# A decoder layer whose sigmoid gates move from classical products inside the merge loop to 14 Strassen units after the gated linear units

## Chip, core and metric

One core of a Trainium2 chip runs the whole layer in one launch. The metric is the device time in microseconds (us). Lower is better.

## What is computed

The layer takes x (1, 512, 2048) in float32. Cut to what matters here:

```
h = rms_norm(x, norm_mix_pre)
q, k, v, u, gate_a, gate_s = jnp.split(h @ w_in, IN_SPLITS, axis=-1)     # gates: 2048 columns each
...
attn_branch = attn.reshape(bsz, s, ATTN_OUT_WIDTH) @ w_attn_up           # 512 -> 2048
y = jax.nn.gelu(s5_ssm(u, ...))                                          # 1024 wide
ssm_branch = (y @ w_glu_v) * jax.nn.sigmoid(y @ w_glu_g)                 # 1024 -> 2048, twice
merged = jax.nn.sigmoid(gate_a) * attn_branch + jax.nn.sigmoid(gate_s) * ssm_branch
x = x + rms_norm(merged @ w_out, norm_mix_post)                          # 2048 -> 2048
h = rms_norm(x, norm_ffn_pre)
f = (jax.nn.silu(h @ w_ffn_gate) * (h @ w_ffn_up)) @ w_ffn_down
return x + rms_norm(f, norm_ffn_post)
```

## The kernel before

**Precision.** Every large product is done three times over: each operand is split into a high part (`_hi`, written by ScalarE as an fp32r copy) and the rest (`_lo`, written by VectorE as raw minus high), and TensorE accumulates hi*hi, hi*lo and lo*hi. The activations stay in SBUF as `a_hi`, `a_lo` (16 tiles of 128 features by 512 tokens) and, for the gated linear units, `y_hi`, `y_lo` (8 tiles). The weights stream from DRAM.

**Pieces.** A piece is 512 KB of weights (four row tiles by 256 columns for `piece_f`; two by 512 for `piece_t`). SP loads it into one of four `raw` slots (`load`), ScalarE splits it (`split_hi`: it waits until piece m-2 is done, since the high parts have two slots), VectorE follows (`split_lo`), and TensorE runs 24 matmuls that stream 512 columns each. So splits of a piece are made while TensorE works on the piece ahead of it. All orders are written out by hand, one list per engine, tied by semaphores; each engine works off its list in order.

**Merge.** Output features are taken in 8 pairs of tiles (256 features, all 512 tokens). Pair 0 of both gates (8 pieces, `B_G0`), the attention output for all pairs (8 pieces, `B_AU`, left in `mrg`) and four pieces of the gated linear unit (`B_Y0`) come first. A loop over `it` = 1 to 7 then runs 12 pieces per pair: four for gate_a, four for gate_s, four for the two halves of the gated linear unit. `gate_glu` takes the sigmoids on ScalarE, `merge` and `merge_attention` multiply and add on VectorE in place in `mrg`. The last turns split `mrg` into `a_hi`, `a_lo` for w_out (`mrg_split_hi`, `mrg_split_lo`), 32 pieces of `piece_t` (`B_WO`).

**Strassen units.** The feed-forward part already does 10 of its 11 column groups as units: 256 output features by 512 tokens by 2048 inputs, as 7 products (`unit_product`, p = 0 to 6) of 8 inner tiles by 3 matmuls that stream 256 columns each: 168 matmuls. Sums of weight quarters are made on VectorE (`block_sum`, four a unit), split operands by `operand_hi` on ScalarE and `operand_lo` on VectorE (seven a unit, into a ring of four slots), the output quarters are put together from PSUM by five small VectorE operations (p = 3, 5, 6 and the next unit's p = 0) and two ScalarE ones. The sums of the activations are made once ahead (`sums`). Even units go with `w_ffn_gate`, odd ones with `w_ffn_up`; each odd one's product is taken by `gate_times_up` in the next unit.

## Time and profile before

| | |
|---|---|
| median of three runs | 2783.3 us (2783.28 to 2784.62) |
| the profiled execution, its own time | 2784.49 us |
| its span from first to last instruction | 2782.7 us |
| TensorE busy | 2733.8 us, 98% |
| VectorE, ScalarE, GpSimd busy | 1307.5, 901.8, 370.2 us |
| mean granted TensorE clock | 0.994 of full |

The page is that of one profiled execution. Busy times of TensorE overlap, so what counts for it is the distance of the starts of consecutive matmuls, and where it sat idle. The other engines' busy shares tell only whether they could be in the way; whether they are is read where an engine waits.

### The profile page before, as it was taken

What the parts mean: (1) busy time and instruction counts of PE and PEld (TensorE: products, weight loads), DVE (VectorE), ACT (ScalarE), POOL (GpSimd) and SP (SyncE); (2) the same over time, 40 slices, a digit from 0 to 9 for tenths busy, and PEclk for the clock granted to TensorE, in tenths of its full rate; (3) what the DMA queues carried; (4) which work ended last, traced back from release to release, by engine and by line L of the source; (5) the groups of instructions that cost most, each with busy time, mean ns of one, the idle gap of its engine ahead of it and who ended that gap; (6) DMA issues with size and microseconds to landing.
All of it is one profiled execution on the core that took longest, in us unless ns stands there. A gap on an engine that the chain in (4) does not pass through costs nothing.

```text
span 2782.7 us, 42515 instructions
## 1 busy us (share of the span) xinstructions
PE 2733.8 (98%) x16733; PEld 2424.5 (87%) x16733; DVE 1307.5 (47%) x1458; ACT 901.8 (32%) x1122; POOL 370.2 (13%) x579
## 2 busy tenths in 40 slices
PE   7999999999999999999799999999999999999998
PEld 6888888888888888888589999999999998888887
DVE  5232332233322223332476777777777773334334
ACT  5222322232322222232333434343433342223223
POOL 5958017761000000000000000000000000000000
PEclk9999999999999999999899999999999999999999
DMA  6444643246233332343334333333334246444443
GB/s 174 141 135 131 126 132 94 92 82 154 91 98 98 98 94 95 98 174 98 105 112 132 106 126 107 118 124 106 127 106 136 98 133 229 141 143 147 147 144 132
DMA packets 256750, 342.46 MB, mean 123 GB/s; under 512 B 22656, under 2 KB 212160, under 8 KB 255520
## 3 DMA queue, kind: packets, MB, share of 16 engines
q1 hardware_dynamic: 232232, 287.89, 32.6%
q0 software_dynamic: 7152, 35.07, 4.7%
q10 hardware_dynamic: 17288, 18.40, 1.9%
q8 instruction: 56, 0.92, 0.1%
q14 instruction: 22, 0.18, 0.0%
HBM read 309.40 MB, written 31.92 MB: 123 GB/s over the span
## 4 chain that ended last, share of the span: by engine, by line
PE 96%; DVE 2%; ACT 1%; issue 1%; DMA 0%; POOL 0%; ACTq 0%; DVEq 0%
PE ps L380 12%; PE ps L382 12%; PE ps L384 12%; PE ps L553 10%; PE ps L551 10%; PE ps L554 10%; PE ps L589 5%; PE ps L587 5%; PE ps L588 5%; PE ps L441 2%; PE ps L439 2%; PE ps L440 2%; PE ps L420 2%; PE ps L424 2%; PE ps L422 2%
## 5 line engine op out<-in xcount | busy, mean ns | idle before, releaser
L368 DVE TENSOR_TENSOR w_lo<-raw,w_hi 128x1024 fp32r<-128x1024 f32 x240 | 308.8, 1287 | 745.6 <-ACT w_hi L364 745.2
L364 ACT ACTIVATE w_hi<-raw 128x1024 fp32r<-128x1024 f32 x240 | 254.1, 1059 | 765.7 <-PE ps L384 532.5
L380 PE MATMUL ps<-a_hi,w_hi 128*128 128x512 f32 x1136 | 445.4, 392 | 1.2 <-issue 1.2
L382 PE MATMUL ps<-a_lo,w_hi 128*128 128x512 f32 x1136 | 442.7, 390 | 0.0
L384 PE MATMUL ps<-a_hi,w_lo 128*128 128x512 f32 x1136 | 442.6, 390 | 0.0
L380 PEld LDWEIGHTS ps<-a_hi,w_hi 128*128 128x128 f32 x1136 | 213.4, 188 | 47.5 <-issue 3.7
L384 PEld LDWEIGHTS ps<-a_hi,w_lo 128*128 128x128 f32 x1136 | 213.3, 188 | 44.3
L382 PEld LDWEIGHTS ps<-a_lo,w_hi 128*128 128x128 f32 x1136 | 213.5, 188 | 43.1
L551 PE MATMUL ps<-a_hi,w_hi 128*128 128x256 f32 x640 | 181.4, 284 | 0.0
L553 PE MATMUL ps<-a_lo,w_hi 128*128 128x256 f32 x640 | 181.4, 283 | 0.0
L554 PE MATMUL ps<-a_hi,w_lo_b 128*128 128x256 f32 x640 | 181.4, 283 | 0.0
L551 PE MATMUL ps<-a_hi,w_hi_b 128*128 128x256 f32 x640 | 181.4, 283 | 0.0
L553 PE MATMUL ps<-a_lo,w_hi_b 128*128 128x256 f32 x640 | 181.4, 283 | 0.0
L554 PE MATMUL ps<-a_hi,w_lo 128*128 128x256 f32 x640 | 181.4, 283 | 0.0
L564 DVE TENSOR_TENSOR f_lo<-f_raw,f_hi 128x512 fp32r<-128x512 f32 x84 | 58.2, 693 | 260.9 <-ACT f_hi L560 260.9
L560 ACT ACTIVATE f_hi<-f_raw 128x512 fp32r<-128x512 f32 x84 | 53.0, 631 | 309.3 <-PE ps L589 309.3
L553 PE MATMUL ps<-s_lo,w_hi_b 128*128 128x256 f32 x480 | 136.1, 284 | 0.0
L554 PE MATMUL ps<-s_hi,w_lo_b 128*128 128x256 f32 x480 | 136.1, 283 | 0.0
L553 PE MATMUL ps<-s_lo,w_hi 128*128 128x256 f32 x480 | 136.1, 283 | 0.0
L554 PE MATMUL ps<-s_hi,w_lo 128*128 128x256 f32 x480 | 136.1, 283 | 0.0
L551 PE MATMUL ps<-s_hi,w_hi 128*128 128x256 f32 x480 | 136.1, 283 | 0.0
L551 PE MATMUL ps<-s_hi,w_hi_b 128*128 128x256 f32 x480 | 136.1, 283 | 0.0
(320 smaller groups left out, 6375.4 us busy)
## 6 DMA issues: line engine op xcount, KB each, us to landing
raw<-in_w_in SPq DMA_DIRECT2D x152, 512.0 KB, 3.6
raw<-in_w_ffn_gate SPq DMA_DIRECT2D x88, 512.0 KB, 4.6
raw<-in_w_ffn_down SPq DMA_DIRECT2D x88, 512.0 KB, 3.7
raw_b<-in_w_ffn_up SPq DMA_DIRECT2D x80, 512.0 KB, 5.2
f_raw<-f_d SPq DMA_DIRECT2D x88, 256.0 KB, 2.7
raw<-in_w_out SPq DMA_DIRECT2D x32, 512.0 KB, 3.8
f_d<-f_t ACTq DMA_DIRECT2D x22, 512.0 KB, 2.8
raw<-in_w_glu_v SPq DMA_DIRECT2D x16, 512.0 KB, 3.4
```

Of the source, the lines that this page charges most:

```text
L364: nc.scalar.activation(w_hi[:, m % 2, :], raw[:, m % 4, :], ACT.Copy).then_inc(hi_ready, 1)
L368: nc.vector.tensor_tensor(w_lo[:, m % 2, :], raw[:, m % 4, :], w_hi[:, m % 2, :].bitcast(F32), ALU.subtract).then_inc(lo_ready, 1)
L380: nc.tensor.matmul(o, wh[:, k, cols], x_hi[:, kt0 + k, :], start=first and k == 0, stop=False, skip_group_check=halves)
L382: nc.tensor.matmul(o, wh[:, k, cols], x_lo[:, kt0 + k, :], start=False, stop=False, skip_group_check=halves)
L384: mm = nc.tensor.matmul(o, wl[:, k, cols], x_hi[:, kt0 + k, :], start=False, stop=last and k == 3, skip_group_check=halves)
L551: nc.tensor.matmul(o, wh[:, k, :], X_HI[p][:, k, :], start=p < 4 and k == 0, stop=False, skip_group_check=True)
L553: nc.tensor.matmul(o, wh[:, k, :], X_LO[p][:, k, :], start=False, stop=False, skip_group_check=True)
L554: mm = nc.tensor.matmul(o, wl[:, k, :], X_HI[p][:, k, :], start=False, stop=k == KT // 2 - 1, skip_group_check=True)
L564: nc.vector.tensor_tensor(dst, f_raw[:, n % 4, :], hi.bitcast(F32), ALU.subtract).then_inc(f_lo_ready, 1)
L587: nc.tensor.matmul(o, f_hi[n % 2][:, toks], wh[:, d, :], start=first, stop=False)
L588: nc.tensor.matmul(o, f_hi[n % 2][:, toks], wl[:, d, :], start=False, stop=False)
L589: mm = nc.tensor.matmul(o, f_lo[n % 2][:, toks], wh[:, d, :], start=False, stop=last)
```

## The change

Pair 0 of the gates stays classical. All 32 pieces of the gated linear unit now run in a row after the attention output; their results go pair by pair through `sig_g` to DRAM (`gl_d`), and the attention output (`mrg`, pairs 1 to 7) goes to DRAM (`au_d`) once, both by GpSimd's queue. In the gaps VectorE and ScalarE make the activation sums for Strassen (`gate_sums`, `gate_sum_hi`), partly in the memory of `mrg`. The seven other pairs of both gates then run as 14 units (`MIX`): even j is gate_a, odd j gate_s. In p = 2 of the odd unit the attention chunk `au_c`, read back from DRAM, is scaled by sigmoid(gate_a) (`merge_attention`); in p = 2 of the unit after it the chunk `gl_c` is scaled by sigmoid(gate_s) and added (`merge_ssm`); the sum goes from `au_c` to DRAM (`m_d`), and only when that has landed is the next `au_c` read. In the last unit `mrg` is read back in two transfers (2 MB and 1.5 MB) as its memory comes free, and the last pair is put into `mrg` straight from VectorE. The output banks of w_out change places. The feed-forward units keep their code, now with `FFN` as the parameter and other semaphore counts.

```diff
-B_WO = B_MRG + 7 * 12
+B_WO = B_Y0 + 4 * 8
 B_FF = B_WO + 32
 B_DN = B_FF + 16
-UNITS = 4 * (FFG - 1)
-DN_USED = 2 * (FFG - 1)
+MIX_UNITS = 2 * 7
+UNITS = MIX_UNITS + 4 * (FFG - 1)
+DN_USED = MIX_UNITS // 2 + 2 * (FFG - 1)
 PROD0 = 4
 LO0 = 8
...
-MRG_RUNS = ((0, 4), (4, 8), (8, 12), (12, 14), (14, 16))
+MRG_RUNS = ((0, 2), (2, 4), (4, 8), (8, 12), (12, 14), (14, 16))
 
...
-            for k in range(4):
-                load(sp, B_Y0 + k, 0, (w_gv, w_gg)[k // 2], 4, 4 * P * (k % 2), 0, 256)
-            with sp.Fori(2, 9) as it:
-                for k in range(12):
-                    if k < 8:
-                        src = (w_in, 4, 4 * P * (k % 4), 256 * it + (GA_COL, GS_COL)[k // 4] - 256, 256)
-                    else:
-                        src = ((w_gv, w_gg)[k // 2 - 4], 4, 4 * P * (k % 2), 256 * it - 256, 256)
-                    load(sp, B_MRG + k - 24, 3 * it, *src)
+            for it in range(8):
+                for k in range(4):
+                    load(sp, B_Y0 + 4 * it + k, 0, (w_gv, w_gg)[k // 2], 4, 4 * P * (k % 2), 256 * it, 256)
+            with sp.Fori(0, 3) as g:
+                for j in range(4):
+                    load_unit(sp, MIX, g, j, w_in, 512 * g + (GA_COL, GS_COL)[j % 2] + 256 * (j // 2 + 1))
+            for j in range(2):
+                load_unit(sp, MIX, 3, j, w_in, (GA_COL, GS_COL)[j] + 256 * 7)
+            sp.wait_ge(unit_lo, LO0 + 7 * (MIX_UNITS - 1))
             with sp.Fori(0, 2) as it:
                 for k in range(16):
                     load(sp, B_WO + k, 4 * it, w_out, 2, 2 * P * (k % 8), 1024 * it + 512 * (k // 8), 512)
...
             pe.wait_ge(au_copied, 8)
             pe.wait_ge(gelu_lo, SSM // P)
-            for k in range(4):
-                piece_f(pe, B_Y0 + k, 0, k // 2 + 2, y_hi, y_lo, 4 * (k % 2), k % 2 == 0, k % 2 == 1)
-            with pe.Fori(1, 8) as it:
-                for k in range(12):
-                    if k < 8:
-                        if k % 4 == 0:
-                            pe.wait_ge(gated, START - 2 + 3 * it + k // 4)
-                        piece_f(pe, B_MRG + k - 12, 3 * it, k // 4, a_hi, a_lo, 4 * (k % 4), k % 4 == 0, k % 4 == 3)
-                    else:
-                        if k == 8:
-                            pe.wait_ge(merge_step, START - 2 + 4 * it)
-                        if k == 10:
-                            pe.wait_ge(gated, START + 3 * it)
-                        piece_f(pe, B_MRG + k - 12, 3 * it, k // 2 - 2, y_hi, y_lo, 4 * (k % 2), k % 2 == 0, k % 2 == 1)
-            pe.wait_ge(gated, START + 23)
+            for it in range(8):
+                for k in range(4):
+                    if it >= 2 and k == 0:
+                        pe.wait_ge(gl_made, it - 1)
+                    if it >= 2 and k == 2:
+                        pe.wait_ge(gated, START + it + 1)
+                    piece_f(pe, B_Y0 + 4 * it + k, 0, 2 * ((it + 1) % 2) + k // 2, y_hi, y_lo, 4 * (k % 2), k % 2 == 0,
+                            k % 2 == 1)
+            with pe.Fori(0, 3) as g:
+                for j in range(4):
+                    for p in range(7):
+                        unit_product(pe, MIX, g, j, p)
+            for j in range(2):
+                for p in range(7):
+                    unit_product(pe, MIX, 3, j, p)
+            pe.wait_ge(c12_made, START + MIX_UNITS - 1)
+            pe.wait_ge(c21_made, START + MIX_UNITS - 1)
             with pe.Fori(0, 2) as it:
                 for k in range(16):
-                    if k in (0, 2, 4, 6, 7):
-                        pe.wait_ge(mrg_lo, (k + 1) // 2 + 1)
+                    if k in (0, 1, 2, 4, 6, 7):
+                        pe.wait_ge(mrg_lo, (0, 1, 2, 4, 6, 7).index(k) + 1)
                     if k == 8:
-                        pe.wait_ge(merge_step, START + 32)
+                        pe.wait_ge(m_made, 7)
+                        pe.wait_ge(c11_read, START + MIX_UNITS)
+                        pe.wait_ge(c12_made, START + MIX_UNITS)
+                        pe.wait_ge(c21_made, START + MIX_UNITS)
                     if k % 8 == 0:
                         pe.wait_ge(o_copied, START - 1 + 2 * it + k // 8)
-                    piece_t(pe, B_WO + k, 4 * it, 4 * (k // 8), a_hi, a_lo, 2 * (k % 8), k % 8 == 0, k % 8 == 7)
...
+                if k >= 8:
+                    c = (k - 8) // 12
+                    if k - 7 - 12 * c in (4, 6, 7, 10):
+                        gate_sum_hi(c, (4, 6, 7, 10).index(k - 7 - 12 * c))
+            act.wait_ge(piece_done, B_WO - 1)
+            operand_hi(act, MIX, 0, 0, 0)
+            act.wait_ge(piece_done, B_WO)
+            operand_hi(act, MIX, 0, 0, 1)
+            operand_hi(act, MIX, 0, 0, 2)
+            gate_glu(7)
...
+            for j in range(2):
+                for p in range(7):
+                    mix_product(3, j, p, False, j == 1)
+            split_hi(act, B_WO + 1, 0)
+            for part in range(2):
+                gate_sigmoids(MIX_UNITS - 1, 1, part)
+            for i in (2, 3, 4):
+                mrg_split_hi(i)
+            split_hi(act, B_WO + 2, 0)
+            mrg_split_hi(5)
...
+            def glu(it):
+
+                dve.wait_ge(gated, START + it + 3)
+                step = tt(sig_g[:, :], pair(2 * ((it + 1) % 2)), sig_g[:, :], ALU.mult)
+                step.then_inc(gl_made, 1)
+                if it == 0:
+                    dve.wait_ge(gl_made, 1)
+                    tt(sig_s[:, :], sig_g[:, :], sig_s[:, :], ALU.mult).then_inc(merge_step, 1)
+                    dve.wait_ge(merge_step, START + 2)
+                    tt(m0, m0, sig_s[:, :], ALU.add).then_inc(merge_step, 1)
...
+            def merge_ssm(g, j, out):
+
+                u = MIX.at(g, j)
+                dve.wait_ge(gl_in, 32 * g + 16 * (j // 2 + 1))
+                dve.wait_ge(gate_sig, 2 * u + 2)
+                dve.wait_ge(c11_read, START + u + 1)
+                tt(gl_c[:, :, :], gl_c[:, :, :], sg[1][:, :, :], ALU.mult).then_inc(gl_scaled, 1)
+                dve.wait_ge(gl_scaled, 2 * g + (j // 2 + 1))
+                dve.wait_ge(au_scaled, 2 * g + (j // 2 + 1))
+                tt(out, au_c[:, :, :], gl_c[:, :, :], ALU.add).then_inc(m_made, 1)
+
+            def merge_attention(g, j):
+
+                u = MIX.at(g, j)
+                dve.wait_ge(au_in, 32 * g + 16 * (j // 2 + 1))
+                dve.wait_ge(gate_sig, 2 * u)
+                dve.wait_ge(c11_read, START + u)
+                tt(au_c[:, :, :], au_c[:, :, :], sg[0][:, :, :], ALU.mult).then_inc(au_scaled, 1)
+
...
-                        merge_attention(it)
-            for k in range(1, 13):
-                split_lo(dve, B_MRG - 12 + k, 21)
-                if k <= 3:
-                    merge(6, k)
-                if k == 8:
-                    merge_attention(7)
-                if k >= 9:
-                    mrg_split_lo(k - 9)
-            for k in range(1, 33):
+            dve.wait_ge(gs_lo_ready, 8)
+            block_sum(MIX, 0, 0, 1)
+            operand_lo(dve, MIX, 0, 0, 0)
+            block_sum(MIX, 0, 0, 3)
+            operand_lo(dve, MIX, 0, 0, 1)
+            block_sum(MIX, 0, 0, 2)
+            glu(7)
+            for j in range(4):
...
+                for p in range(7):
+                    mix_product(3, j, p, False, j == 1)
+            mix_c21(MIX_UNITS - 1, 1)
+            split_lo(dve, B_WO + 1, 0)
+            mrg_split_lo(2)
+            merge_ssm(3, 1, mrg[:, KT - 2:KT, :])
+            mrg_split_lo(3)
+            mrg_split_lo(4)
+            split_lo(dve, B_WO + 2, 0)
+            mrg_split_lo(5)
+            for k in range(3, 33):
                 split_lo(dve, B_WO + k, 0)
-                if k <= 3:
-                    merge(7, k)
-                if k == 4:
-                    mrg_split_lo(4)
                 if k in (9, 17, 25):
                     out_gain((k - 9) // 8)
...
 
 
-            pool.wait_ge(mrg_lo, 5)
+            pool.wait_ge(au_copied, 8)
+            pool.dma_start(au_d[:, 2:KT, :], mrg[:, 2:KT, :]).then_inc(au_stored, 16)
+            pool.wait_ge(merge_step, START + 3)
+            pool.dma_start(m_d[:, 0:2, :], mrg[:, 0:2, :]).then_inc(m_stored, 16)
+            for it in range(1, 8):
+                pool.wait_ge(gl_made, it + 1)
+                pool.dma_start(gl_d[:, 2 * it:2 * it + 2, :].rearrange("p a n -> p (a n)"), sig_g[:, :]
+                               ).then_inc(gl_stored, 16)
+            for it in range(1, 8):
+                kts = slice(2 * it, 2 * it + 2)
+                if it > 1:
+                    pool.wait_ge(m_made, it - 1)
+                    pool.dma_start(m_d[:, 2 * it - 2:2 * it, :], au_c[:, :, :]).then_inc(m_stored, 16)
+                    pool.wait_ge(m_stored, 16 * it)
+                else:
+                    pool.wait_ge(gs_lo_ready, 8)
+                    pool.wait_ge(au_stored, 16)
+                pool.dma_start(au_c[:, :, :], au_d[:, kts, :]).then_inc(au_in, 16)
+                pool.wait_ge(gl_stored, 16 * it)
+                pool.dma_start(gl_c[:, :, :], gl_d[:, kts, :]).then_inc(gl_in, 16)
+            pool.wait_ge(product, PROD0 + 7 * MIX_UNITS - 5)
+            pool.dma_start(mrg[:, 0:8, :], m_d[:, 0:8, :]).then_inc(mrg_in[0], 16)
+            pool.wait_ge(product, PROD0 + 7 * MIX_UNITS - 4)
+            pool.dma_start(mrg[:, 8:14, :], m_d[:, 8:14, :]).then_inc(mrg_in[1], 16)
+
```

Two places on VectorE, as the program lists them. In names, buffer numbers left out, `w_lo` and `mix_lo_b` are the four slots of the ring for low parts; what stands in brackets is what the operation waits for. The first place is where the classical pieces end and the units begin, now (the row at the top splits the last piece of the gated linear unit):

```order
L417 TENSOR_TENSOR w_lo<-raw,w_hi 128x1024 [waits hi_ready]
L1797 TENSOR_TENSOR gs_lo_145<-gs_tmp_150,gs_hi_142 128x1024 [waits gs_hi_ready]
L1846 TENSOR_TENSOR mix_t_sum<-raw 128x1024 [waits landed1,landed0,gs_lo_ready]
L566 TENSOR_TENSOR w_lo<-raw,w_hi 128x1024 [waits unit_hi]
L1849 TENSOR_TENSOR raw<-raw 128x8x128 [waits landed3,landed2]
L566 TENSOR_TENSOR w_lo<-raw,w_hi 128x1024 [waits unit_hi]
L1852 TENSOR_TENSOR raw<-raw 128x8x128 [waits t_made]
L1778 TENSOR_TENSOR sig_g<-ps,sig_g 128x1024 [waits gated]
L566 TENSOR_TENSOR mix_lo_b<-raw,mix_hi_b 128x1024 [waits unit_hi] x2
```

The product of the last gated linear unit (L1778) stands between the second operand's low part and the third's. ScalarE's list at the same place, from the high part of operand 0 to that of operand 3, has its sigmoid (L1278) there too:

```order
L561 ACTIVATE w_hi<-raw 128x1024 [waits landed1,product,landed0,piece_done]
L561 ACTIVATE w_hi<-raw 128x1024 [waits landed3,product,landed2,piece_done]
L561 ACTIVATE mix_hi_b<-raw 128x1024 [waits product,t_made]
L1278 ACTIVATE sig_g<-ps 128x1024 [waits piece_done,gl_stored]
L561 ACTIVATE mix_hi_b<-raw 128x1024 [waits product,t_made]
```

The sigmoid comes behind operand 2's high part there, while on VectorE the product that needs it comes ahead of operand 2's low part. The last place is VectorE at the start of w_out. Before, the splits of w_out's weights (L368) and the last merge's steps and splits took turns:

```order
L1682 TENSOR_TENSOR a_lo<-mrg,a_hi 128x1024 [waits mrg_hi]
L368 TENSOR_TENSOR w_lo<-raw,w_hi 128x1024 [waits hi_ready]
L1653 TENSOR_TENSOR sig_g<-ps,sig_g 128x1024 [waits gated]
L368 TENSOR_TENSOR w_lo<-raw,w_hi 128x1024 [waits hi_ready]
L1656 TENSOR_TENSOR sig_g<-sig_g,sig_s 128x1024 [waits merge_step]
L368 TENSOR_TENSOR w_lo<-raw,w_hi 128x1024 [waits hi_ready]
L1659 TENSOR_TENSOR mrg<-mrg,sig_g 128x1024 [waits merge_step]
```

Now (from the split of w_out's first piece, the first L417, on; the second L417 splits its second piece, the third its third):

```order
L417 TENSOR_TENSOR w_lo<-raw,w_hi 128x1024 [waits hi_ready]
L1859 TENSOR_TENSOR sg_157<-mix_u_159,ps 128x256 [waits product]
L417 TENSOR_TENSOR w_lo<-raw,w_hi 128x1024 [waits hi_ready]
L1939 TENSOR_TENSOR a_lo<-mrg,a_hi 128x2048 [waits mrg_hi]
L1867 TENSOR_TENSOR gl_c<-gl_c,sg_157 128x1024 [waits c11_read,gate_sig,gl_in]
L1870 TENSOR_TENSOR mrg<-au_c,gl_c 128x1024 [waits au_scaled,gl_scaled]
L1939 TENSOR_TENSOR a_lo<-mrg,a_hi 128x2048 [waits mrg_hi]
L1939 TENSOR_TENSOR a_lo<-mrg,a_hi 128x1024 [waits mrg_hi]
L417 TENSOR_TENSOR w_lo<-raw,w_hi 128x1024 [waits hi_ready]
```

Five operations of VectorE stand between the low parts of w_out's second and third piece, where before one stood between two neighbours.

## Rows read from the trace of the kernel before

**Rows 1.** The page: span and busy time of each engine.

```profile
span 2782.7 us, 42515 instructions
...
PE 2733.8 (98%) x16733; PEld 2424.5 (87%) x16733; DVE 1307.5 (47%) x1458; ACT 901.8 (32%) x1122; POOL 370.2 (13%) x579
```

**Rows 2.** Busy time by window: merge from the first B_Y0 piece; feed-forward units.

```profile
717.50:1196.40 478.90, 478.85 (x2112) 396.82 (x2113) 147.76 (x120) 119.08 (x113) 0.00 (x0) 1.00 0.31 96
1488.50:2294.90 806.40, 806.40 (x6721) 806.36 (x6721) 604.40 (x659) 325.91 (x403) 0.00 (x0) 1.00 0.36 119
```

**Rows 3.** Waits of TensorE from 718 to 1370 us: total, times, longest.

```profile
PE ps L380 <- ACT mrg L1208: 1.1, 1, 1.1
```

**Rows 4.** Timeline of VectorE: end of an odd unit, an even unit from 1851.4.

```profile
1840.10 0.42 DVE L1812 TENSOR_TENSOR u_s<-p_s,ps 128x256 f32<-128x256 f32 x1 [3.04 <-PE ps L554]
...
1855.91 1.22 DVE L1791 TENSOR_TENSOR f_t<-f_t,f_sg 128x1024 f32<-128x1024 f32 x1
1857.05 1.22 DVE L519 TENSOR_TENSOR w_lo<-t_sum,w_hi 128x1024 fp32r<-128x1024 f32 x1
1860.35 0.42 DVE L1812 TENSOR_TENSOR u_s<-p_s,ps 128x256 f32<-128x256 f32 x1 [2.08 <-PE ps L554]
```

**Rows 5.** Timeline of ScalarE in the odd unit from 1831.3.

```profile
1834.22 0.62 ACT L1301 ACTIVATE f_sg<-f_sg 128x512 f32<-128x512 f32 x1
...
1835.70 0.40 ACT L1301 ACTIVATE f_sg<-f_sg 128x256 f32<-128x256 f32 x1
```

**Rows 6.** Timeline of TensorE and ScalarE where product 3 of a unit ends.

```profile
1822.61 0.28 PE L551 MATMUL ps<-a_hi,w_hi_b 128*128 128x256 f32 x1
...
1822.83 1.06 ACT L514 ACTIVATE w_hi<-raw 128x1024 fp32r<-128x1024 f32 x1 [4.71 <-PE ps L554]
```

**Rows 7.** Chain of waits: VectorE's split, then 0.14 us until TensorE starts.

```profile
709.37 1.23 DVE w_lo L368
710.60 0.14 issue
```

**Rows 8.** Operations on mrg: durations in ns, min/median/max.

```profile
L1208 ACT ACTIVATE mrg<-ps x8: 1023/1025/1026, 667.6 to 716.5; 128x1024 f32<-128x1024 f32 x8
...
L1659 DVE TENSOR_TENSOR mrg<-mrg,sig_g x8: 1216/1218/1219, 752.8 to 1209.8; 128x1024 f32 x6, 128x1024 f32<-128x1024 f32 x2
L1227 ACT ACTIVATE a_hi<-mrg x5: 1044/1902/1907, 1176.7 to 1213.9; 128x2048 fp32r<-128x2048 f32 x3, 128x1024 fp32r<-128x1024 f32 x2
L1682 DVE TENSOR_TENSOR a_lo<-mrg,a_hi x5: 1217/2291/2293, 1178.7 to 1215.2; 128x2048 fp32r<-128x2048 f32 x3, 128x1024 fp32r<-128x1024 f32 x2
```

**Rows 9.** DMA issues: count, KB each, median us from issue to landing.

```profile
h_r<-h_d POOLq DMA_DIRECT2D x8, 512.0 KB, 14.7
...
x_d<-x POOLq DMA_DIRECT2D x1, 4096.0 KB, 11.4
x_b<-x_d POOLq DMA_DIRECT2D x1, 4096.0 KB, 17.8
```

**Rows 10.** Windows (us, PE, PEld, DVE, ACT, POOL busy, TensorE's clock, DMA).

```profile
1370.00:1371.00 1.00, 0.64 (x3) 0.19 (x1) 0.00 (x0) 0.32 (x1) 0.00 (x0) 1.00 0.55 194
...
1372.00:1373.00 1.00, 0.00 (x0) 0.00 (x0) 0.00 (x0) 1.00 (x4) 0.00 (x0) 0.89 0.00 0
1373.00:1374.00 1.00, 0.00 (x0) 0.00 (x0) 0.83 (x3) 0.98 (x3) 0.00 (x0) 0.50 0.00 0
...
1396.00:1397.00 1.00, 1.00 (x8) 1.00 (x7) 0.90 (x2) 0.83 (x2) 0.00 (x0) 0.66 0.01 0
```

**Rows 11.** Timeline of TensorE at half clock, and the restart at 1392.6.

```profile
25.10 0.41 PE L403 MATMUL ps<-a_lo,w_hi 128*128 128x256 f32 x1
25.32 0.41 PE L405 MATMUL ps<-a_hi,w_lo 128*128 128x256 f32 x1
...
1392.62 8.83 PE L709 MATMUL ps<-ident,o_t 128*128 128x128 f32 x61 [0.72 <-DVE o_t L1719]
```

475 lines of the change are left out of this document (322 added, 153 removed).

## The prediction

> **What bounds the kernel now.** First the page's busy times: TensorE is busy 2733.8 of 2782.7 us, VectorE 47%, ScalarE 32% [rows 1]. The reader is to see that only TensorE can set the time as a whole; a change helps by giving it less to stream, and hurts by making it wait. Then the busy time by window, for the stage that is changed: from 717.50 to 1196.40 us, TensorE runs 2112 matmuls of 512 columns without a gap, one every 478.85/2112 = 0.2267 us. VectorE is busy 147.8 us of that, DMA 31% [rows 2]. Its waits in this stage come to 1.1 us in all, once, for ScalarE's last copy of the attention output [rows 3]; the change leaves that one in place. The same view of the feed-forward units gives 6720 matmuls of 256 columns in 806.4 us: 0.1200 us each, again without a gap, with VectorE at 604.4/806.4 = 75% [rows 2]. So both forms of work are in the trace, at full clock.
>
> **The change part by part.** *Removed and added products.* A gate's pair of tiles took 4 pieces, 96 matmuls of 0.2267: 21.77 us. As a unit it takes 168 of 0.1200: 20.16 us, the same for any unit, since 40 of them took 806.4. 14 x 1.61 = 22.5 us less. The 32 pieces of the gated linear units are the same matmuls as before; only their order changes.
> The Trainium skill's page "TensorE: Matmul & The Clock Gate", section "Back-to-back issue gap", has a matmul cost its columns over 2.4 GHz and 2.5 ns: 109 ns for 256 columns, 216 for 512. By that a unit would be 18.3 us, four pieces 20.7, and 14 of them would save 33 us. The rows show 120 and 227 ns, so the sum goes by them.
>
> *Work that TensorE hides.* Ahead of the units VectorE does 24 sums of 1024 elements and ScalarE 8 copies, at most one each a piece, behind the piece's split. A VectorE operation of that size starts 1.14 us after the one ahead of it (1855.91, 1857.05) and takes 1.22 [rows 4]; a piece on TensorE is 24 x 0.2267 = 5.44 us, and split, sum and the pair's product come to 3.6. Nothing. If the cover went, a sum would cost 1.14 us a time.
> In the units, VectorE has what it has in the feed-forward units plus, in p = 2, one operation of 1.22 in an odd unit (there was none) and two in an even one (there was one, L1791). What they eat into is its idle time ahead of p = 3: 3.04 us in an odd unit, 2.08 in an even one [rows 4]. 3.04 - 1.2 leaves 1.8. In the even one the sigmoids come in: ScalarE now takes them in every unit, 0.62 and 0.40 [rows 5], which puts operand 4's high part some 0.6 later, and the add must wait for the scaling, so 2.08 - 1.2 - 0.2 leaves near 0.6 at best and near nothing at worst. VectorE then starts p = 3's sum when product 3 is done, as now, 2.2 us before TensorE needs it (the sum ends at 1860.77; the unit began at 1822.61 - 4 x 2.88 + 2 x 20.16 = 1851.41 [rows 6], its product 4 starts 11.52 later). Nothing, in all 14 units.
>
> *Two places where the cover is gone.* **The first unit.** Call T0 the end of the last classical piece. The high part of operand 1 goes into the slot that piece used, operand 2's where `y_hi` lay, so both come after T0. ScalarE sees an end of products about 0.25 after the next matmul could start (1822.83 against 1822.61 [rows 6], somewhat more with 512 columns). ScalarE 0.25 to 1.31 (1.05 for 1024 elements, 0.96 from start to start of two); VectorE's low part to 2.57, its third sum to 3.71; ScalarE's operand 2 to 4.88, its sigmoid to 5.81 (1.03, as L1208 [rows 8]); VectorE's product of the gated linear unit to 7.07, and only then operand 2's low part, to 8.22. From such an end to TensorE's start is 0.14 [rows 7]: 8.36, where product 2 was due at 2 x 2.88 = 5.76. A stall of 2.6 us. Behind that row wait TensorE and VectorE's operand 3, which is done at 9.4, before product 3.
> **w_out's third piece.** Call T1 the end of the last unit. ScalarE: split of the second piece to 1.31, two sigmoids to 2.15, the 2048-element high part to 3.95 (1.90 [rows 8]). VectorE: 1.35 to 2.58, low part 3.97 to 6.26 (2.29), scaling and adding the last pair to 8.67, a low part of 2048 and one of 1024 to 12.02, and then the third piece's split, to 13.17. TensorE starts it at 13.3; it was due at T1 + 10.88. A stall of 2.4 us. The fourth piece is due 5.44 later and needs two more operations: no stall. Before, single operations stood between the splits and nothing waited. Together 5.0 us; as bounds, 0 if work TensorE has queued covers it, 7 if each chain is a microsecond longer than its sum.
>
> *The clock.* TensorE's last matmul before the end of w_out ends at 1370.64. The window from 1372 shows 0.89, the one from 1373 0.50 of the clock, that is 1.2 GHz: it fell some 2.1 us into the idle time, after a long dense stretch. It came back in the window from 1396, 4.1 us after TensorE's long run began at 1392.62 [rows 10, 11]. Both stalls are a little longer than 2.1. At half clock, matmuls of 256 columns start every 0.21 us instead of 0.12 [rows 11]; 4.1 us of that lose 4.1 x (1 - 0.12/0.21) = 1.8 us. The other end of the bound is nothing, as the 1.1 us stall at 716 cost nothing more. I take one fall of the two, 1.8; the bounds are 0 and 3.6.
>
> *DMA.* Through GpSimd's queue go 3.5 MB at the start of the linear units, then 0.5 MB a pair, and 1.5 MB for each pair of units. On it 4096 KB left SBUF in 11.4 us and came back in 17.8 with 1 MB ahead of it [rows 9]. The slots run three pieces ahead (16 us), so a weight load that lands ten us later still makes it. The last unit's 2 MB read is issued at its 6.0 us and is wanted at 14.6; half of 11.4 and half of 17.8 are 5.7 and 8.9, so it lands at 11.7 to 14.9: nothing to 0.6 us. Nothing.
>
> *Sum.* -22.5 + 5.0 + 1.8 = -15.7 us. The profiled execution took 2784.49, so its like would take 2768.8, with a span of 2767.0; the median of the runs is 1.2 below it, and 2783.3 - 15.7 = 2767.6.
>
> **The rivals.** Under 0.2% (5.6 us) is about what a measurement of this kernel can't tell from no change.
> *No stall shows (12%).* Queued work covers both places, or the clock holds and one of them is hidden. For it: in all units so far TensorE never waited. Against it: the sums above have no slack. 2783.3 - 22.5 = 2760.8, up to 2763.
> *The reload is late (10%).* ScalarE's wait for `mrg` stands in front of w_out's first split. If the 2 MB take as long per byte as 512 KB of `h_r` did amid other traffic, 14.7 [rows 9], they land 6 us late: 2767.6 + 6 = 2774.
> *The trip through DRAM sets the pace of the units (5%), the slower side.* One buffer, `au_c`: the sum is made about 8.3 us into an even unit, stored, waited for, and the next chunk read into it, wanted 5.7 us into the next unit; with 4 us that VectorE and TensorE can bear, 20.2 + 5.7 - 8.3 + 4 = 21.6 us for two transfers. At 3 to 5 us each they take under half. At 14.7 each, as `h_r`, 29.4: 7.8 late, six times, 47 us, so 2767.6 + 47 = 2815. It decides above (15.7/6 + 21.6)/2 = 12.1 us a transfer. Against: DMA is busy 36% in the feed-forward units [rows 2]. The Trainium skill's page "SBUF — State Buffer", section "SBUF: two separate sides", speaks for it: transfers issued by GpSimd's queue starve while VectorE holds the port they share in its fast two-port mode. No row here shows such a case.
> *256 columns go at half of 512's time (2%)*, 0.1134: 14 x (21.77 - 19.05) = 38 saved, 2752. The 806.4 us speak against it.
> The remaining 6% is for a wait that I have not seen, which takes most of the gain.
>
> **How the numbers follow.** Forecast 65%, with its own range 2763.5 to 2770. The range reaches to full gain below, 2760.8, and into the late reload above: 2761 to 2773, which leaves out the slow trip, the fast matmuls and the unseen. Faster by over 0.2%: 65 + 12 + 10 + 2 = 89, and 1 of the unseen; within 0.2%: 4; slower: 6.
>
> **What would show it.** Right: 168 matmuls a unit in 20.16 us from about 892; TensorE idle 2.6 us once, two products later, released by VectorE's `mix_lo_b`, and 2.4 us, two pieces into w_out, released by `w_lo`; from w_out's first matmul at 1176 to 1178 on, the rest as before, shifted. Wrong: waits of TensorE inside the loop of units, VectorE waiting for `au_c` or `gl_c`, or ScalarE for `mrg`; a clock of 0.50 for longer than 4 us after a stall; a distance other than 0.120.

## The result and the profile after

The changed kernel takes 2767.3 us (median of four runs, 2766.4 to 2769.7) against 2783.8 for the kernel before, run beside it: a ratio of 0.9942, 95% interval 0.9925 to 0.9959, 16.5 us or 0.6% less. The forecast was 2767.6. The profiled executions differ by 18.0 us in their spans (2782.7 [rows 1] and 2764.7); what the sum of terms has to explain is those 18.0. It said 15.7. (One execution of the kernel with the late reload, 2973.4 us at a mean granted clock of 0.85, and one of the kernel before, 3892.8 us at 0.65, are slow ones and stand in no comparison below.)

The page of the changed kernel, its span and busy times:

```profile
span 2764.7 us, 44896 instructions
...
PE 2712.5 (98%) x17741; PEld 2453.8 (89%) x17741; DVE 1471.9 (53%) x1651; ACT 955.3 (35%) x1215; POOL 386.4 (14%) x610
```

TensorE has 1008 matmuls more and 21.3 us less to do; VectorE has 164 us more to do, and TensorE's waits below are all that shows of it. The busy times by window, for the 14 units, from there to the feed-forward units, and the feed-forward units (columns as in [rows 10]):

```profile
890.80:1175.60 284.80, 282.61 (x2354) 282.27 (x2352) 227.35 (x243) 120.41 (x155) 12.16 (x23) 1.00 0.46 155
1175.60:1470.50 294.90, 272.37 (x1218) 225.83 (x1218) 133.34 (x104) 96.66 (x121) 1.59 (x3) 0.96 0.35 120
1470.50:2276.90 806.40, 806.40 (x6722) 806.40 (x6721) 604.52 (x659) 325.05 (x403) 0.00 (x0) 1.00 0.36 119
```

The first row is to be read against 14 x 20.16 = 282.24: 2352 matmuls, 120.0 ns each, and 2.5 us beside them. The third is for TensorE the row of before [rows 2]: nothing changed there, it is only earlier. TensorE's waits, in us: total, times, longest. Of the kernel before, the same view had neither of the first two rows:

```profile
PE ps L604 <- DVE mix_lo_b L566: 2.2, 1, 2.2
PE ps L488 <- DVE w_lo L417: 1.9, 1, 1.9
...
PE ps L429 <- ACT mrg L1266: 1.1, 1, 1.1
```

Those are the two stalls of the forecast, at its places and with its releasers. TensorE's timeline: the first matmul of the units, the one that ends the first stall, w_out's first, and the one that ends the second stall:

```profile
890.79 0.28 PE L604 MATMUL ps<-a_hi,w_hi 128*128 128x256 f32 x1
...
898.89 0.38 PE L604 MATMUL ps<-gs_hi,mix_hi_b 128*128 128x256 f32 x1 [2.19 <-DVE mix_lo_b L566]
...
1175.55 0.50 PE L488 MATMUL ps<-w_hi,a_hi 128*128 128x512 f32 x1
...
1188.68 0.50 PE L488 MATMUL ps<-w_hi,a_hi 128*128 128x512 f32 x1 [1.95 <-DVE w_lo L417]
```

Product 2 was due at 890.79 + 5.76 = 896.55 and came at 898.89, 2.34 late. The third piece was due at 1175.55 + 11.02 (two pieces with the stretched first matmul; 10.9 of matmuls) and came 2.1 late. The number in brackets is smaller, since it counts from the end of the matmul ahead, and a matmul's row is 0.28 us long where the starts lie 0.12 apart.

VectorE's rows show the order that holds each of them up: the product of the last gated linear unit (L1778) ahead of operand 2's low part, and two low parts of merged chunks ahead of the third piece's (the last row):

```profile
896.48 1.23 DVE L1778 TENSOR_TENSOR sig_g<-ps,sig_g 128x1024 f32<-128x1024 f32 x1 [2.04 <-ACT sig_g L1278]
897.62 2.35 DVE L566 TENSOR_TENSOR mix_lo_b<-raw,mix_hi_b 128x1024 fp32r<-128x1024 f32 x2
...
1184.07 3.42 DVE L1939 TENSOR_TENSOR a_lo<-mrg,a_hi 128x2048 fp32r<-128x2048 f32 x2
1187.41 1.22 DVE L417 TENSOR_TENSOR w_lo<-raw,w_hi 128x1024 fp32r<-128x1024 f32 x1
```

And the clock, windows of 1 us around both stalls (the value after POOL's busy time):

```profile
897.00:898.00 1.00, 0.00 (x0) 0.00 (x0) 1.00 (x2) 1.00 (x2) 0.00 (x1) 1.00 1.09 350
898.00:899.00 1.00, 0.11 (x1) 0.11 (x2) 1.00 (x2) 1.00 (x3) 1.00 (x2) 1.00 0.61 195
899.00:900.00 1.00, 1.00 (x9) 1.00 (x10) 1.00 (x2) 0.56 (x1) 0.58 (x2) 1.00 0.94 378
...
1188.00:1189.00 1.00, 0.32 (x1) 0.30 (x2) 1.00 (x2) 0.00 (x0) 0.00 (x0) 1.00 0.00 0
1189.00:1190.00 1.00, 1.00 (x6) 0.81 (x5) 1.00 (x2) 0.00 (x0) 0.00 (x0) 1.00 0.18 27
```

In these and all windows beside them it stayed at 1.00, that is 2.4 GHz. The forecast had 1.8 us for one fall; in this execution there was none.

### The profile page after: what moved, and what is told of

Its sections match the earlier page's. It is cut to its first block, busy times and chain, and to the rows that moved or that the text cites. A ratio compares the mean times of both kernels' runs of the same rounds, so it can differ in the third digit from the quotient of the medians.

```text
span 2764.7 us, 44896 instructions
## 1 busy us (share of the span) xinstructions
PE 2712.5 (98%) x17741; PEld 2453.8 (89%) x17741; DVE 1471.9 (53%) x1651; ACT 955.3 (35%) x1215; POOL 386.4 (14%) x610
## 4 chain that ended last, share of the span: by engine, by line
PE 96%; DVE 2%; ACT 1%; issue 1%; ACTq 0%; DVEq 0%
PE ps L604 13%; PE ps L607 13%; PE ps L606 13%; PE ps L429 8%; PE ps L431 8%; PE ps L433 8%; PE ps L640 6%; PE ps L642 6%; PE ps L641 6%; PE ps L488 2%; PE ps L489 2%; PE ps L490 2%; PE ps L469 2%; PE ps L473 2%; PE ps L471 2%
## 5 line engine op out<-in xcount | busy, mean ns | idle before, releaser
L417 DVE TENSOR_TENSOR w_lo<-raw,w_hi 128x1024 fp32r<-128x1024 f32 x184 | 240.4, 1306 | 538.4 <-ACT w_hi L413 538.0
L429 PE MATMUL ps<-a_hi,w_hi 128*128 128x512 f32 x688 | 270.6, 393 | 1.2 <-issue 1.2
L431 PE MATMUL ps<-a_lo,w_hi 128*128 128x512 f32 x688 | 267.9, 389 | 0.0
L433 PE MATMUL ps<-a_hi,w_lo 128*128 128x512 f32 x688 | 267.9, 389 | 0.0
L606 PE MATMUL ps<-a_lo,w_hi 128*128 128x256 f32 x872 | 246.8, 283 | 0.0
L607 PE MATMUL ps<-a_hi,w_lo 128*128 128x256 f32 x872 | 246.8, 283 | 0.0
L604 PE MATMUL ps<-a_hi,w_hi 128*128 128x256 f32 x872 | 246.8, 283 | 0.0
L606 PEld LDWEIGHTS ps<-a_lo,w_hi 128*128 128x128 f32 x872 | 167.4, 192 | 0.0
L604 PEld LDWEIGHTS ps<-a_hi,w_hi 128*128 128x128 f32 x872 | 167.4, 192 | 0.0
L607 PEld LDWEIGHTS ps<-a_hi,w_lo 128*128 128x128 f32 x872 | 167.4, 192 | 0.0
L429 PEld LDWEIGHTS ps<-a_hi,w_hi 128*128 128x128 f32 x688 | 129.2, 188 | 29.9 <-issue 3.7
L433 PEld LDWEIGHTS ps<-a_hi,w_lo 128*128 128x128 f32 x688 | 129.1, 188 | 27.0
L431 PEld LDWEIGHTS ps<-a_lo,w_hi 128*128 128x128 f32 x688 | 129.2, 188 | 25.9
```

Of the source, the lines that this page charges most:

```text
L417: nc.vector.tensor_tensor(w_lo[:, m % 2, :], raw[:, m % 4, :], w_hi[:, m % 2, :].bitcast(F32), ALU.subtract).then_inc(lo_ready, 1)
L429: nc.tensor.matmul(o, wh[:, k, cols], x_hi[:, kt0 + k, :], start=first and k == 0, stop=False, skip_group_check=halves)
L431: nc.tensor.matmul(o, wh[:, k, cols], x_lo[:, kt0 + k, :], start=False, stop=False, skip_group_check=halves)
L433: mm = nc.tensor.matmul(o, wl[:, k, cols], x_hi[:, kt0 + k, :], start=False, stop=last and k == 3, skip_group_check=halves)
L604: nc.tensor.matmul(o, wh[:, k, :], ph.x_hi[p][:, k, :], start=p < 4 and k == 0, stop=False, skip_group_check=True)
L606: nc.tensor.matmul(o, wh[:, k, :], ph.x_lo[p][:, k, :], start=False, stop=False, skip_group_check=True)
```

## The experiments

Every kernel here is the changed one with the edit shown. "Units" is the time from the first unit's first matmul to w_out's first, 284.76 us in the changed kernel; "w_out" from there to the first feed-forward unit, 294.93 (292.14 before). Medians are compared with the changed kernel's 2767.3, which was measured in the first set alone; the kernel before, run beside every set, had medians from 2783.5 to 2784.3. So a difference of under 1 us between medians tells nothing here, and the traces decide on the small ones.

### Is each stall the order of a queue?

In the first unit, the last gated linear unit goes behind operand 3, on ScalarE and on VectorE:

```diff
             operand_hi(act, MIX, 0, 0, 2)
-            gate_glu(7)
...
                     operand_hi(act, MIX, g, j, p + 3)
+                    if first and p == 0:
+                        gate_glu(7)
...
-            glu(7)
...
                     operand_lo(dve, MIX, g, j, 3)
+                    if first:
+                        glu(7)
```

> The changed kernel with one edit: the sigmoid and the product of the last gated linear unit stand behind operand 3 of the first unit, not ahead of operand 2's low part. Theory A (the 2.35 us stall at the first unit's product 2 is the queue order of ScalarE and VectorE, and nothing else): operand 2's low part then starts when its high part is ready, at about 895.5 in the changed kernel's trace, ends 896.7, TensorE starts product 2 at about 896.9, due 896.54: a stall of some 0.3 us is left, 2.0 us less, 2765.2 from 2767.2. Rival B (something queued behind makes up for it, for instance the first unit's q waits for the store of the last linear unit, which is now later): less than 1 us gained, and a new wait of TensorE at product 5 or at the second unit. Rival C (the stall costs more than its length by the clock): over 3 us gained.

2764.4 us (2763.7 to 2765.7, 5 runs), 2.8 less; the profiled spans are 2.0 apart (2762.7 and 2764.7). The units took 282.64 us, 2.12 less, and TensorE's wait for `mix_lo_b` is off the list. But w_out took 296.24, 1.31 more. The windows behind the third piece's stall, which was 2.15 us long by the same row, show why:

```profile
1185.00:1186.00 1.00, 0.48 (x2) 0.38 (x3) 1.00 (x2) 0.00 (x0) 0.00 (x0) 0.87 0.00 0
1186.00:1187.00 1.00, 1.00 (x4) 0.81 (x3) 1.00 (x2) 0.00 (x0) 0.11 (x1) 0.50 0.15 49
1187.00:1188.00 1.00, 1.00 (x4) 0.80 (x3) 0.73 (x1) 0.00 (x0) 0.94 (x2) 0.50 0.91 272
...
1189.00:1190.00 1.00, 1.00 (x6) 0.83 (x5) 0.00 (x0) 0.00 (x0) 0.00 (x0) 0.93 0.97 381
```

Here the clock did fall, to 1.2 GHz, for some 3 us, in which the matmuls of 512 columns start 0.43 us apart in place of 0.227. It fell at 1185.7, just behind the stall's end at 1185.52. The hundredth matmul behind the stall comes 24.40 us after it, in the changed kernel 22.80: the fall cost 1.6. (The 1.31 is less, since the restart behind w_out was 0.46 quicker here.) Theory A holds for the stall; the clock term that the changed kernel's profile did not have is back at the other stall, which the edit does not touch.

At w_out, the third piece's split goes ahead of the parts of the merged chunks that are wanted only at its fifth, seventh and eighth pieces (much the same on ScalarE):

```diff
             mrg_split_lo(2)
             merge_ssm(3, 1, mrg[:, KT - 2:KT, :])
+            split_lo(dve, B_WO + 2, 0)
             mrg_split_lo(3)
             mrg_split_lo(4)
-            split_lo(dve, B_WO + 2, 0)
-            mrg_split_lo(5)
             for k in range(3, 33):
                 split_lo(dve, B_WO + k, 0)
+                if k == 3:
+                    mrg_split_lo(5)
```

> The changed kernel with one edit: the split of w_out's third piece stands ahead of the high and low parts of the merged chunks 8 to 14, and the last chunk pair's part behind the fourth piece's split. Theory A (the 2.1 us stall at the third piece is the VectorE list): VectorE ends the third piece's split about 9.9 us after the last unit, TensorE wants it at 10.9: no stall, 2.1 us less, 2765.1 from 2767.2. Rival B (the low parts moved back now come late themselves, at the fourth or fifth piece): VectorE reaches the fourth piece's split about 14.5 us after the last unit, wanted at 16.3; if each operation took 0.5 us longer it would be late, and under 1 us would be gained.

2765.1 us (2762.7 to 2765.4, 5 runs), 2.2 less. The wait at L488 is gone and no other has come; w_out took 292.09. VectorE's timeline in that stretch (1174.73 is w_out's first matmul):

```profile
1182.19 1.23 DVE L1872 TENSOR_TENSOR mrg<-au_c,gl_c 128x1024 f32<-128x1024 f32 x1
1183.34 1.22 DVE L417 TENSOR_TENSOR w_lo<-raw,w_hi 128x1024 fp32r<-128x1024 f32 x1
1184.47 3.42 DVE L1941 TENSOR_TENSOR a_lo<-mrg,a_hi 128x2048 fp32r<-128x2048 f32 x2
1187.81 1.22 DVE L417 TENSOR_TENSOR w_lo<-raw,w_hi 128x1024 fp32r<-128x1024 f32 x1
```

The third piece's low part ends at 1184.56, wanted at 1174.73 + 10.9 = 1185.6; the fourth's ends at 1189.03, wanted 5.44 later, at 1191.1.

Both edits, and the fourth sum of the first unit ahead of operand 1's low part, so that operand 2's high part need not wait for it:

> The changed kernel with both edits (the last gated linear unit behind operand 3, the third piece's split first) and the fourth sum of the first unit (raw) ahead of operand 1's low part. Theory A (both stalls are queue order only, and add up): TensorE without a wait from the linear units to the end of w_out, 2.35 + 2.1 = 4.45 us less than the changed kernel, 2762.8, a span of 2760.2; ratio to the kernel before 0.9924. Rival B (a stall that goes lets the next limit show, as the reload of 2 MB with no spare): w_out's start is late by up to 1 us.

2762.1 us (2761.4 to 2764.6, 5 runs), ratio to the kernel before 0.9922 (0.9909 to 0.9936): 5.2 less than the changed kernel. Its windows for the units and for w_out:

```profile
891.10:1173.30 282.20, 282.20 (x2353) 282.20 (x2352) 226.11 (x242) 120.41 (x155) 12.16 (x23) 1.00 0.47 157
1173.30:1465.50 292.20, 271.60 (x1219) 225.22 (x1218) 133.15 (x104) 96.45 (x121) 1.59 (x3) 0.96 0.36 121
```

TensorE is busy every one of the 282.2 us, and w_out takes what it took before the change. Both stalls were queue order, and what they cost adds up (2.8 and 2.2 by the medians alone, 5.2 together); this is the fastest version of the study.

### Is the gain TensorE's columns, or the new order?

TensorE does 14 times 96 matmuls of 512 columns in place of 14 times 168 of 256. What this kernel leaves out is the gates' values: it is there for its time only.

```diff
+            if ph is MIX:
...
+                count = 14 if p < 5 else 13
+                for n in range(count):
+                    k = n // 3
+                    wt = wl if n % 3 == 2 else wh
+                    xt = a_lo if n % 3 == 1 else a_hi
+                    mm = nc.tensor.matmul(wide, wt[:, k, :], xt[:, KT // 2 + k, :], start=p < 4 and n == 0,
+                                          stop=n == count - 1, skip_group_check=True)
...
```

> The changed kernel, except that each of the 14 units has TensorE do 96 matmuls of 512 columns (on other tiles, so the gates' values are not computed) in place of 168 of 256, with everything else of the units left: the column count of the classical form within the new order. Theory A (the gain is TensorE's columns alone, 1.61 us a unit, and the reordering itself is worth nothing or a little): 14 x (21.77 - 20.16) = 22.5 us more than the changed kernel, 2789.8, so 6 us above the kernel before, which is the two stalls and what goes with them. Rival B (part of the gain comes from the reordering, as merged chunks out of the way): less than 2783.3. Rival C (VectorE at 80% and DMA set the units' pace, so that TensorE's columns are partly hidden): the units take less than 14 x 21.77 = 304.8 us plus the stall.

2790.1 us (11 runs, 2788.0 to 2790.9), 22.8 more than the changed kernel and 6 above the kernel before (ratio 1.0020, 1.0011 to 1.0029). The units took 306.53 in place of 284.76, with everything else of VectorE, ScalarE and the trips through DRAM left in:

```profile
890.80:1197.40 306.60, 305.01 (x1346) 252.25 (x1345) 228.48 (x243) 121.89 (x155) 12.16 (x23) 1.00 0.43 144
```

The first stall is 1.75 us here, since the two products ahead of it are longer; 306.53 less that is 304.8, which is 14 x 21.77. Theory A holds for the columns: they give 22.5 back. What the order alone costs is less sure: 6 us by the medians, 3.5 by the profiled spans (2786.2 and 2782.7), and that profile is of the fastest of the 11 runs. Rival B, a gain from the order, is out either way.

### Does the clock fall in such a stall?

VectorE gets one or four operations of 1024 elements more, ahead of the last gated linear unit's product.

```diff
             block_sum(MIX, 0, 0, 2)
+            for _ in range(1):                # 4 in the second kernel
+                link(tt(gs_tmp[1][:, :, :], gs_tmp[2][:, :, :], gs_tmp[2][:, :, :], ALU.subtract))
             glu(7)
```

> The changed kernel with one more VectorE operation of 1024 elements ahead of the last gated linear unit's product, so that TensorE's stall at the first unit's product 2 grows from 2.35 to about 3.6 us. Theory A (the clock falls when TensorE has stood for some 2.1 us, as in the stall after w_out and in the run with the last gated linear unit moved, where the window behind the 2.15 us stall shows 0.66; it stayed at 1.00 here only because 2.2 us of waiting are at the edge): 1.2 for the longer stall and 1.8 for the clock, 3.0 us more, 2770.2, and windows of 0.50 for some 4 us behind the stall. Theory B (a single gap in this stretch does not bring the clock down): 1.2 us more, 2768.5, and 1.00 throughout.

> The same with four operations ahead: a stall of about 7.2 us. Theory A (one fall and one return, whatever the length of the stall): 4.8 for the stall and 1.8 for the clock, 6.6 us more, 2773.9. Theory B (the clock stays): 4.8 more, 2772.1. Rival C (the longer the stall, the longer the half clock behind it): over 8 us more.

2767.9 us (2767.3 to 2768.4) and 2772.4 us (2772.3 to 2773.0), 4 runs each: 0.6 and 5.1 more. The expectation had left something out: VectorE stood idle for 2.04 us at this very place, waiting for the sigmoid, so that one operation fits in for nothing. The stall was 2.41 us from due to start with one operation (2.26 in the row), 5.25 with four. But in the profiled execution of the first the clock fell:

```profile
898.00:899.00 1.00, 0.50 (x4) 0.50 (x5) 1.00 (x2) 1.00 (x2) 1.00 (x3) 1.00 0.44 165
899.00:900.00 1.00, 1.00 (x9) 1.00 (x8) 1.00 (x2) 0.10 (x1) 0.20 (x1) 0.71 1.03 393
900.00:901.00 1.00, 1.00 (x7) 1.00 (x6) 0.72 (x1) 0.00 (x0) 0.00 (x0) 0.50 0.83 107
...
902.00:903.00 1.00, 1.00 (x7) 1.00 (x7) 0.00 (x0) 0.00 (x0) 0.00 (x0) 0.58 1.06 422
903.00:904.00 1.00, 1.00 (x11) 1.00 (x10) 0.83 (x2) 0.00 (x0) 0.00 (x0) 1.00 0.64 254
```

and this stall is the changed kernel's but for 0.07 us. The units took 286.23: over 282.24 and the stall's 2.41, and the 0.17 that the changed kernel has there too, that leaves 1.4 us for the clock. With four operations the units took 289.89, which leaves 2.2, and the windows show 0.50 from 901 to 907. So there was one fall and one return each time, as A has it, at 1.4 and 2.2 us, where the prediction had 1.8. But the half clock did last longer behind the longer stall, some 6 us for some 3, which is rival C's mechanism at a far smaller price. And A's condition, that 2.1 us of standing bring the fall, does not hold: see the clock's term below. In the medians the longer stall alone, with the 2.04 us of idle time taken off, explains 0.1 of the 0.6 and 2.9 of the 5.1. The second leaves room for the clock's 2.2; the first is too small to tell how often it fell in the runs without a trace.

### Has the reload from DRAM time to spare?

```diff
-            pool.wait_ge(product, PROD0 + 7 * MIX_UNITS - 5)
+            pool.wait_ge(product, PROD0 + 7 * MIX_UNITS - 4)     # and -3 for the second load
```

> The changed kernel with both loads of the merged tiles issued one product (2.88 us) later. Theory A (the 2 MB reload has no spare time: it landed 0.4 us behind the moment that ScalarE could have used it, and w_out began 0.05 us behind the first piece's low part): w_out begins 2.9 us later after the last unit, the lists of ScalarE and VectorE behind it move with it, so the stall at the third piece stays: 2.9 us more, 2770.1; if ScalarE's wait for the product stood ahead all the same, some tenths less. Theory B (the chain through the splits sets w_out's start, the reload only seems to): under 1 us more.

2766.5 us (2766.4 to 2767.9, 3 runs), as the changed kernel: theory A's 2770.1 failed, and B's number came true, though not for B's reason. TensorE's timeline:

```profile
1177.27 0.50 PE L488 MATMUL ps<-w_hi,a_hi 128*128 128x512 f32 x1 [1.49 <-DVE w_lo L417]
...
1189.05 0.50 PE L488 MATMUL ps<-w_hi,a_hi 128*128 128x512 f32 x1 [0.61 <-DVE w_lo L417]
```

w_out starts 1.5 us late, not 2.9, since this load took 7.7 us from issue to ScalarE's start where the other took 9.0; and what is lost there comes back at the third piece, whose wait falls from 1.95 to 0.61. Two waits one behind the other don't add: the third piece's chain on VectorE starts with the end of the last unit, and a late start of w_out is time in which it runs. The test of that is the same edit on the kernel that has no stall at the third piece:

> The kernel with both orders mended (TensorE without a wait in these stages), and both loads of the merged tiles one product (2.88 us) later. In the changed kernel that cost w_out's start 1.5 us, which came back at the third piece, whose 1.95 us of waiting became 0.6: that chain starts from the end of the last unit, not from w_out's start. Theory A (two delays overlap there, and the reload has some 1.4 us of slack against its issue, since it landed in 7.7 us in place of 9.0): with no stall at the third piece to take it, the 1.5 us stay: 2762.1 + 1.5 = 2763.6. Theory B (the reload doesn't matter for the end whatever the order): 2762.1.

2762.7 us (2761.7 to 2764.0, 4 runs), within the scatter of the 2762.1 without it. The profiled execution shows the 1.5 us (units 283.74 against 282.23, a wait of 1.35 at w_out's first matmul) and w_out at 292.36. By the trace A holds; the medians, 0.6 apart, can't tell A from B.

### How near is the trip through DRAM to setting the pace?

Three more transfers of 512 KB, one after another, in each of the six trips, and then two:

```diff
                     pool.wait_ge(m_stored, 16 * it)
+                    for n in range(3):        # 2 in the second kernel
+                        pool.dma_start(pad_d[:, n, :, :], au_c[:, :, :]).then_inc(padded, 16)
+                        pool.wait_ge(padded, 16 * (3 * (it - 2) + n + 1))
```

> The changed kernel with three more transfers of the 512 KB chunk, one after another, between the store of the merged chunk and the load of the next one, six times. The trip took 2.9 + 4.0, with waits 7.4 us, and would take some 17. Theory A (the prediction's bound: 21.6 us from the sum to the next chunk's use, 4 of them spare time on VectorE and TensorE): hidden, 2767.3 within 1 us. Theory B (what is hidden ends where VectorE wants the chunk, 17.6 us after the sum, or earlier, because VectorE at 80% has no spare time): VectorE waits for the chunk and TensorE loses up to 2 us at six places.

2782.7 us (10 runs, 2779.7 to 2786.2): 15.4 more, so both theories were too small. GpSimd's timeline of the first trip (in brackets what it waited for), and VectorE's first use of the chunk:

```profile
943.07 0.54 POOL L2361 DMA_DIRECT2D m_d<-au_c  x1 [43.68 <-DVE au_c L1872]
946.25 0.54 POOL L2364 DMA_DIRECT2D pad_d<-au_c  x1 [2.64 <-DMA m_d<-au_c]
949.42 0.53 POOL L2364 DMA_DIRECT2D pad_d<-au_c  x1 [2.64 <-DMA pad_d<-au_c]
956.39 0.53 POOL L2364 DMA_DIRECT2D pad_d<-au_c  x1 [6.44 <-DMA pad_d<-au_c]
960.73 0.54 POOL L2369 DMA_DIRECT2D au_c<-au_d  x1 [3.80 <-DMA pad_d<-au_c]
...
964.70 1.23 DVE L1880 TENSOR_TENSOR au_c<-au_c,sg 128x1024 f32<-128x1024 f32 x1 [4.17 <-DMA au_c<-au_d]
```

A transfer took 3.2 us where the queues were quiet and 7.0 where a unit's weights came in (9.3 at worst in a later trip). The whole trip is 21.6 us and VectorE waited 4.2 for it; TensorE had no wait at its next sum, but one of 0.5 us eight us later. The six trips took 21.4 to 22.8. Behind the two up to 21.6 TensorE lost 0.5 and 0.7, behind those of 21.9 to 22.8 up to 2.2 at once; in all it waited 8.4 us in eight places, VectorE up to 6.2 at a time. In three of seven windows of 40 us the clock shows 0.96: one fall behind the first unit's stall, which this edit does not touch, and two behind waits of 1.75 and 2.20 us. So a trip of 21.6 us, the prediction's bound, was just borne; and 17 expected us had become 21.6, because a transfer takes not 3.4 us but 3.2 to 9.3.

> The changed kernel with two more transfers in the trip through DRAM, one after another. With three, the first trip took 943.07 to 964.7, 21.6 us, and TensorE had no wait at it though VectorE waited 4.2; later ones took up to 6.2 us more than VectorE had, and the kernel lost 15.4 us. Theory A (the prediction's bound of 21.6 us from the sum to the chunk's use is right, and only my 3.4 us a transfer was low: they take 3.2 to 8.8 amid the weight loads): a trip of some 17.5 us, VectorE waits little, TensorE not, 2767.3 to 2768. Theory B (every microsecond of VectorE's wait costs TensorE): VectorE's waits and the loss are alike, some 5 us.

2766.9 us (4 runs, 2765.5 to 2767.6): nothing, and no wait of TensorE in the units but the old one. VectorE waited 4.6 us in all, five times, 1.6 at most, at trips of 18.0 to 19.0 us. So not every microsecond of VectorE's wait costs TensorE one: theory B is out. The changed kernel's own trip is 7.4 us.

### How much time has VectorE to spare in a unit?

```diff
                         merge_ssm(*((g, j - 1) if j else (g - 1, 3)), au_c[:, :, :])
+                    for i in range(0 if first or last else 2):       # 4 in the second kernel
+                        tt(pad[:, :, :], a_hi[:, 8:11, quad[0]].bitcast(F32), a_hi[:, 8:11, quad[1]].bitcast(F32), ALU.add
+                           ).then_inc(padded, 1)
+                        dve.wait_ge(padded, 2 * (u - 1) + i + 1)
```

> The changed kernel with two more VectorE operations of 768 elements (about 0.9 us each) ahead of product 3's work in each of the 12 units between the first and the last. It weighs the prediction's 'nothing, in all 14 units'. Theory A (VectorE has the idle time ahead of p = 3, 0.9 us in an even unit and 2.15 in an odd one in the changed kernel, and 2.1 us more until TensorE needs its sum: 8.64 + 0.25 + 0.42 + 0.14 against 11.52 into the unit): 1.8 us is under 3.0 and 4.2, nothing lost, 2767.3. Theory B (VectorE at 80% is nearly a bound, the idle time is broken up by waits for ScalarE that move with it): waits of TensorE in the even units, over 2 us in all.

> The same with four, 3.6 us a unit. Theory A: 3.6 - 3.0 = 0.6 us late in the six even units, hidden in the odd ones: 3.6 us more, 2770.9, TensorE waiting for the sum (mix_u) there; clock as before, since each wait is under 2 us. Theory B (VectorE then has 16.2 + 3.6 = 19.8 of 20.16 us a unit, and no way to catch up): late more and more, over 10 us.

2774.6 us (7 runs, 2772.5 to 2775.6) and 2799.2 us (4 runs, 2798.5 to 2800.4): 7.4 and 31.9 more. Theory A fell, twice. One window over ten units, of the changed kernel:

```profile
930.00:1130.00 200.00, 200.00 (x1669) 200.00 (x1669) 161.51 (x173) 83.86 (x110) 7.93 (x15) 1.00 0.43 143
```

of the kernel with two operations more:

```profile
930.00:1130.00 200.00, 196.87 (x1627) 195.46 (x1626) 174.95 (x189) 79.86 (x107) 7.97 (x15) 1.00 0.43 143
```

and with four:

```profile
930.00:1130.00 200.00, 182.90 (x1480) 179.68 (x1479) 176.85 (x190) 71.94 (x97) 6.90 (x13) 0.99 0.39 129
```

From two to four VectorE's busy time hardly rises, 87% to 88%: that is where it is full. Its waits in the kernel with four (total, times, longest):

```profile
DVE w_lo L568 <- ACT w_hi L563: 19.4, 15, 3.1
DVE mix_lo_b L568 <- ACT mix_hi_b L563: 15.2, 13, 1.2
```

and in the changed kernel:

```profile
DVE mix_u L1899 <- PE ps L607: 20.1, 14, 2.4
DVE w_lo L566 <- ACT w_hi L561: 19.5, 15, 3.1
DVE mix_lo_b L566 <- ACT mix_hi_b L561: 15.3, 13, 1.2
```

The 35 us of waits for ScalarE's high parts are the same in both. They are round trips: VectorE makes a sum, ScalarE rounds it, VectorE takes the low part, and when VectorE is later the round trip is later with it. Only the wait for TensorE's product gives: 0.9 us in an even unit and 2.15 in an odd one, 3.04 for the two, 1.5 a unit. Two operations took 1.97 us: 12 x (1.97 - 1.52) = 5.4; four took 3.96: 12 x 2.44 = 29.3. Measured are 7.4 and 31.9 in the medians, 6.1 and 31.5 in the units of the profiled executions (290.87 and 316.24), and 24.5 between the medians against 23.9. What is above the sum has two sources in the rows, which no run takes apart: the next operation waits for the end of the added ones, 1.7 and 2.2 us in all, and with four operations the clock fell three times in the units, once of it behind the first unit's stall.

## Why the prediction was right, and where it was off

*Fewer columns, -22.5.* Right: 282.24 us for 14 units of 168 matmuls, 282.23 measured without a stall, and 304.8 for 282.24 between the wide and the narrow form without their stalls.

*First unit's stall, 2.6.* It was 2.34. The chain went as worked out, on both engines: the low part began at 897.62, 6.83 us after the classical pieces' end, where the sum of durations had 7.07, since an operation starts some 0.1 us before the one ahead of it is over.

*Third piece's stall, 2.4.* It was 2.1: the low part ended 13.08 us after the last unit for 13.17, and the piece was due 0.14 later than matmuls at full pace have it.

*The clock, 1.8.* This is the term that was mis-sized: 0 in the profiled execution. That such a stall can bring the clock to 1.2 GHz holds; that 2.1 us of standing decide it does not. Seven kernels have the first unit's stall alike, 2.19 us in the row. The clock fell behind it in the profiles of two, those with three more transfers and with four operations a unit, and stayed at 2.4 GHz in five. The stall and a window behind it, with three more transfers:

```profile
898.69 0.39 PE L606 MATMUL ps<-gs_hi,mix_hi_b 128*128 128x256 f32 x1 [2.19 <-DVE mix_lo_b L568]
...
901.00:902.00 1.00, 1.00 (x7) 1.00 (x6) 0.00 (x0) 0.00 (x0) 0.00 (x0) 0.50 0.89 299
```

and the same window of the changed kernel:

```profile
901.00:902.00 1.00, 1.00 (x11) 1.00 (x10) 0.11 (x1) 0.00 (x0) 0.00 (x0) 1.00 0.70 221
```

At the two places together the profiles hold 16 stalls of 1.95 to 2.26 us, and 5 of them have a fall behind them, which came 0.2 to 1.5 us after TensorE had started again. The Trainium skill's page "TensorE: Matmul & The Clock Gate", section "What's actually happening", has the gate judge by windows that run free of the program, so that the same kernel comes out differently from run to run. The rows agree: equal gaps, unequal clocks. The price, from matmul to matmul, is 1.5 us in the units (the hundredth behind the stall comes 13.6 us after it for 12.1) and 1.6 in w_out, with the long stall 2.3. So an estimate of the term is 2/7 x 1.5 + 2/8 x 1.6 = 0.8 us on average, not 1.8: the prediction had one fall in every execution, and there is about one in two.

Without a fall the terms give -22.5 + 2.34 + 2.1 = -18.1, the profiled difference of 18.0. That it fits to a tenth is luck: the scatter below, 1.0 less and 0.6 more, and some 0.4 in small gaps cancel. The medians are 16.5 apart, 1.5 less. Half of that is on the kernel before, whose profiled execution was 0.7 above its median; the other 0.8 is how far the changed kernel's profiled execution, the fastest of four, lies below its median. The estimate of 0.8 fits it. That falls of the clock make it up is argued, not shown: the other executions have no trace. The kernel without stalls gained 5.2 in the median where 4.45 of stalls went, which fits too. That the forecast hit 2767.3 us to 0.3 has luck in it as well: the gain was 16.5 for 15.7, and the kernel before stood 0.5 higher beside it than the 2783.3 that the forecast started from.

*Beside the change.* w_out took 2.8 us more than before; 2.1 are the stall, 0.6 is the run of 61 transposes behind w_out, 9.41 us against 8.83 [rows 11]. In the other kernels, which leave that place alone, it took 8.3 to 9.6. It is scatter of the restart from 1.2 GHz, not the change. The wait of 1.0 us for `t_q` ahead of the linear units was missing in this execution and 0.2 to 0.6 or missing in others: scatter too.

*DMA, nothing.* Right, by luck in one place. The 2 MB load was issued at 6.2 us of the last unit and landed at 15.2, just past the upper end of 11.7 to 14.9, and TensorE began w_out 0.05 us behind VectorE's last low part. The rival "the reload is late" gave 1 us for 1 us; the run with the late reload shows that the stall at the third piece took back 1.3 of 1.5 us.

*The trip through DRAM.* Its bound of 21.6 us was right to a few tenths. Its transfers were taken from the wrong side: 3 to 5 us hold in quiet stretches. Of transfers held back by VectorE nothing shows: it was busy 80% of the units, and the changed kernel's six stores took 2.9 to 3.1 us each to land.

*VectorE's idle time, nothing in all 14 units.* The result was right: no wait of TensorE in the units but the first stall. The margin was not. The prediction added 2.2 us that TensorE can wait for product 4's sum to the idle time ahead of it. That time is to be had once. A delay that comes every unit has only the idle time that VectorE doesn't give back to ScalarE, 1.5 us a unit; the change left that much, and one operation more of 1.22 us in every unit would, as an estimate, have eaten most of it.

## What to carry to other kernels

When work is moved out of a loop, look at its seams first: in the first and the last pass the operation that TensorE wants next goes ahead of all that is wanted later, which here was worth 5 us for a few moved lines. The slack for a cost that recurs is the engine's idle time less the round trips to other engines that move with it, not the room at one deadline. Judge two edits together: a wait that goes may uncover the next, and one that comes may hide in one that is there.

## What the runs showed of the hardware that was not expected

TensorE's clock stayed at 2.4 GHz behind gaps of 1.90 to 2.19 us and fell to 1.2 GHz for some 3 us behind gaps of 1.75 to 2.49 us in other executions, in one and the same place (2.19 us) both ways, at 1.5 or 1.6 us a time where it was measured. In all but one of these nine falls TensorE had started again before it. A store of 512 KB to DRAM through GpSimd's queue took 3.2 us when alone and 7.0 when a unit's four weight loads ran beside it. VectorE was full at 88% busy, with four operations more in a unit.
